# Expert outputs of a mixture-of-experts layer: from a scatter to DRAM and a gather back, to one-hot matmuls that are added to x block by block

## The reference

```python
def hierarchical_moe(h, ...):              # h: 512 tokens x 1024
    g_idx = argmax(h @ w_rg + b_rg)        # 1 of 4 groups
    top_v, top_i = top_k(le[g_idx], 2)     # 2 of its 8 experts
    wts = gate_g * softmax(top_v)
    # the 1024 (token, expert) pairs are sorted by expert
    run_block = (silu(xblk @ w_gate[e]) * (xblk @ w_up[e])) @ w_down[e]   # ff = 512
    out = segment_sum(yb * buf_w, buf_tok)
for i in range(2):
    x = x + mixer_i(rmsnorm(x))
    x = x + hierarchical_moe(rmsnorm(x, norm_ffn_g[i]), ...)
return rmsnorm(x, final_norm_g)
```

## Time and profile before

| | us |
|---|---|
| median of three runs | 1715.41 (1713.95 to 1717.63) |
| the profiled execution, its own time | 1716.26 |
| its span, first to last instruction | 1714.2 |
| expert stage, layer 0 (first gate/up matmul to the end of the last down product) | 477.48 to 939.65 |
| expert stage, layer 1 | 1207.80 to 1685.90 |

### The profile page before, as it was taken

How to read it: one execution, slowest core, us unless ns; L and a number is a source line. 1 busy time by engine, 2 the same in 40 slices (tenths; PEclk the granted TensorE clock), 3 DMA queues, 4 the chain that set the end, 5 groups by cost and what they waited for, 6 DMA issues and landing times. The chain is left out here.

```text
span 1714.2 us, 38730 instructions
## 1 busy us (share of the span) xinstructions
PE 1430.4 (83%) x16146; PEld 929.1 (54%) x16147; DVE 497.1 (29%) x1197; ACT 458.2 (27%) x800; POOL 356.8 (21%) x291
## 2 busy tenths in 40 slices
PE   6999999999796899877588499887977877788883
PEld 5868688686453455444345387565544444445442
DVE  4221121211431222111122779744311211112124
ACT  4242422423321222212122332153212221222222
POOL 3434244342000011100001354520001000001010
PEclk9999999999899999989999699988999998999997
DMA  9212122121779999999999221135499999999985
GB/s 357 99 50 98 50 99 99 49 99 49 294 331 427 429 427 428 428 428 429 429 425 374 99 98 50 52 148 196 170 429 413 413 416 430 427 429 429 416 342 204
DMA packets 39321, 473.83 MB, mean 276 GB/s; under 512 B 6397, under 2 KB 6605, under 8 KB 10849
## 3 DMA queue, kind: packets, MB, share of 16 engines
q1 hardware_dynamic: 34512, 464.42, 65.3%
q0 software_dynamic: 4608, 8.41, 1.3%
q10 hardware_dynamic: 144, 0.17, 0.0%
HBM read 462.48 MB, written 14.68 MB: 278 GB/s over the span
## 5 line engine op out<-in xcount | busy, mean ns | idle before, releaser
L788 PE MATMUL ps<-ring,hgT 128*32 128x256 f32 x6016 | 379.0, 404 | 144.2 <-DMA ring<-w_gu 118.9
L788 PEld LDWEIGHTS ps<-ring,hgT 128*32 128x32 f32 x6016 | 202.4, 115 | 310.3 <-DMA ring<-w_gu 144.9
L437 POOL TENSOR_TENSOR w_lo<-ring,w_hi 128x512 fp32r<-128x512 f32 x176 | 237.5, 1351 | 375.3 <-ACT w_hi L513 375.3
L452 POOL DMA_INDIRECT y_dram<-area_c,idx_s x96 | 94.4, 983 | 781.0 <-ACT area_c L550 761.3
L731 PE MATMUL ps<-area_a,block_rows 128*32 128x256 f32 x3136 | 202.3, 401 | 8.9 <-DVE block_rows L995 8.9
L513 ACT CAST w_hi<-ring 128x512 fp32r<-128x512 f32 x176 | 109.1, 626 | 353.6 <-PE ps L691 353.6
L1117 DVE TENSOR_TENSOR a_e<-sg_e,ps 128x128 f32<-128x128 f32 x94 | 27.1, 288 | 605.8 <-ACT sg_e L545 605.8
L804 PE MATMUL ps<-ring,aT_e 128*32 128x256 f32 x2752 | 166.3, 382 | 25.4 <-DMA ring<-w_down 12.7
L731 PEld LDWEIGHTS ps<-area_a,block_rows 128*32 128x32 f32 x3136 | 111.0, 117 | 83.4 <-issue 26.0
L689 PE MATMUL ps<-w_hi,hT_hi 128*128 128x512 f32 x320 | 126.0, 394 | 7.2 <-DVE hT_lo L1296 7.2
L545 ACT ACT_TABLE_LOAD x94 | 120.6, 1283 | 40.7 <-DVE wts L1111 39.0
(11 more groups left out here) (199 smaller groups left out, 1508.2 us busy)
## 6 DMA issues: line engine op xcount, KB each, us to landing
ring<-w_gu SPq DMA_DIRECT2D x128, 2048.0 KB, 19.0
ring<-w_down SPq DMA_DIRECT2D x58, 2048.0 KB
ring<-w_pw SPq DMA_DIRECT2D x6, 2048.0 KB, 10.9
ring<-w_qk SPq DMA_DIRECT2D x4, 2048.0 KB
ring<-w_v SPq DMA_DIRECT2D x4, 2048.0 KB, 8.2
ring<-w_g SPq DMA_DIRECT2D x4, 2048.0 KB
ring<-w_out SPq DMA_DIRECT2D x4, 2048.0 KB
area_c<-w_down SPq DMA_DIRECT2D x2, 2048.0 KB, 12.6
```

Of the source, the lines that this page charges most:

```text
L437: nc.gpsimd.tensor_tensor(w_lo[:, place, :], ring[:, s, at:at + 512], w_hi[:, place, :].bitcast(F32), ALU.subtract).then_inc(lo_ready, 1)
L452: pool.indirect_dma_start(y_dram[l], bass.IndirectOffsetOnAxis(ap=idx_s[:, b:b + 1].bitcast(U32), axis=0), y_out[:, b, :], None, bounds_ch ...
L788: last = nc.tensor.matmul(ps[32 * g:32 * g + 32, 2, 0:256], hgT[:, n * (KT // 2) + k, :], gate_up[n][:, k, :, g * P:(g + 1) * P], start=(n ...
```

## The change

Nothing goes through DRAM any more. After each block, four one-hot row tiles bring its output to x:

- ACT and DVE write the output, times its routing weight, as the sum of two fp32r parts, `y_hi` (ACT) and `y_lo` (DVE).
- POOL makes `slot_tok` (128 x 512): 1 where slot p of the block holds token t.
- PE does `put_rows` twice per block (halves of 256 tokens): 16 matmuls in fp32r with K = 32 rows, 128 output columns and 256 moving columns each, in four row groups of the array, group g to PSUM bank 4 + g. They run one block late: in block t they move the output of block t-1. The first half stands behind gate/up, the second behind the down product.
- DVE adds each 128 x 1024 row tile from four banks to x (`add_tile`, four per block).
- Picking is one block ahead instead of two, behind the first half of `put_rows`.
- The ring has nine slots, three experts deep (`DEPTH = 3`); the places of the spare down matrices became slots 6 to 8. Now expert 2 is loaded before the stage, nine loads of 96 as before.
- The routing weights are worked out earlier, and the table matmul (L772) has 216 columns in place of 72. After the last block there are two more halves of `put_rows` and four adds, in place of the transfers and `combine`.

```diff
+        places = [ring[:, n, :] for n in range(NSLOT)] + \
+            [area_c[:, 0:SLOT], area_b[:, 0:SLOT], hT[:, :, :].rearrange("p k s -> p (k s)")]
-        slots_of = [(0, 1, 2), (3, 4, 5)]
+        slots_of = [(0, 1, 2), (3, 4, 5), (6, 7, 8)]
@@ SP
-                        upto = sp.value_load(cum[0:1, bass.ds(2 * pair + (odd - 1), 1)], min_val=1, max_val=NBLK - 1)
+                        upto = sp.value_load(cum[0:1, bass.ds(DEPTH * turn + (n - 2), 1)], min_val=1, max_val=NBLK - 1)
-                sp.wait_ge(rows_out[l], 1)
-                for i in range(NT):
-                    sp.dma_start(ytile[i], y_dram[l].rearrange("(t r) c -> t (r c)", r=8)[i * P:(i + 1) * P, :]) \
-                        .then_inc(y_loaded[l][i], 16)
@@ POOL
+                with pool.Fori(0, total) as t:
+                    pool.wait_ge(tok_hot[l], t + 1)
+                    pool.nop(nofuse=True)
+                    pool.tensor_copy(slot_now[:, :], slots[:, bass.ds(t, 1)]).then_inc(slot_known[l], 1)
+                    pool.wait_ge(slot_known[l], t + 1)
+                    pool.wait_ge(second_mm[l], t + 1)
+                    pool.nop(nofuse=True)
+                    nc.gpsimd.tensor_scalar(slot_tok[:, :], tok_number, slot_now[:, 0:1], None,
+                                            ALU.is_equal).then_inc(tok_hot[l], 1)
@@ ACT
                     act.wait_ge(y_mm[l], t + 1)
-                    act.wait_ge(y_free[l], t + 1)
-                    nc.scalar.copy(area_c[:, bass.ds((t % GRP) * QW + 4096, QW)], ps[:, 4, 0:QW]) \
-                        .then_inc(y_ready[l], 1)
+                    act.wait_ge(second_mm[l], t + 1)
+                    nc.scalar.activation(y_hi[:, :], ps[:, 3, P:P + QW], ACT.Copy,
+                                         scale=slots[:, bass.ds(t + NBLK, 1)]).then_inc(y_rounded[l], 1)
@@ PE
+            def put_rows(half, bank, done):
+                for i in range(2):
+                    cols = slice((2 * half + i) * P, (2 * half + i + 1) * P)
+                    for n, part in enumerate((y_hi, y_lo)):
+                        for g in range(4):
+                            rows = slice(32 * g, 32 * g + 32)
+                            last = nc.tensor.matmul(ps[:, bank + g, i * QW:(i + 1) * QW], slot_tok[rows, cols],
+                                                    part[rows, :], start=(i == 0 and n == 0), stop=(i == 1 and n == 1),
+                                                    tile_position=(32 * g, 0))
+                last.then_inc(done, 1)
...
-                pick_rows(l, t + 2)
+                pe.wait_ge(y_split[l], t + 1)
+                pe.wait_ge(tok_hot[l], t + 1)
+                pe.wait_ge(added[l], 4 * t + 4)
+                put_rows(0, 4, first_mm[l])
+                pick_rows(l, t + 1)
                 pe.wait_ge(act_ready[l], t + 1)
                 nc.tensor.transpose(ps[:, 3, 0:P], a_e[:, :], ident).then_inc(t2_mm[l], 1)
                 turn_block(l, t + 1)
...
                 last.then_inc(y_mm[l], 1)
+                pe.wait_ge(added[l], 4 * t + 6)
+                put_rows(1, 4, second_mm[l])
@@ DVE, loop over the blocks
-                    dve.wait_ge(gu_mm[l], t + 1)
+                    dve.wait_ge(first_mm[l], t + 1)
+                    add_tile(0, 4).then_inc(added[l], 1)
+                    stage(l, t + 1)
+                    add_tile(1, 4).then_inc(added[l], 1)
                     turned_block(l, t + 1, gain)
-                    stage(l, t + 2)
-                    know_rows(l, t + 3)
+                    know_rows(l, t + 2)
+                    dve.wait_ge(y_rounded[l], t + 1)
+                    V.scalar_tensor_tensor(out=y_lo[:, :], in0=ps[:, 3, P:P + QW],
+                                           scalar=slots[:, bass.ds(t + NBLK, 1)], in1=y_hi[:, :].bitcast(F32),
+                                           op0=ALU.mult, op1=ALU.subtract).then_inc(y_split[l], 1)
+                    dve.wait_ge(second_mm[l], t + 1)
+                    add_tile(2, 4).then_inc(added[l], 1)
+                    add_tile(3, 4).then_inc(added[l], 1)
```

More of the change, by code:

```diff
@@ L159, in program @@
         slot_hot_r = over("slot_hot_r", [P, 8, P], trig_at, 0)
-        block_hot_r = over("block_hot_r", [P, 8, NBLK], area_c_at, route_at)
+        block_hot_r = over("block_hot_r", [P, 3, 8, NBLK], area_c_at, route_at)
+        y_hi = over("y_hi", [P, QW], area_c_at, route_at)
+        y_lo = over("y_lo", [P, QW], area_c_at, route_at + QW)
+        slot_tok = over("slot_tok", [P, S], area_c_at, route_at + 2 * QW)
         ident = const[:, C_ID:C_ID + P]
@@ L201, in program @@
         eq = room[:, 784:912].rearrange("p (i e) -> p i e", i=NT)
-        block_hot = room[:, 576:1152].rearrange("p (j b) -> p j b", j=8)
-        work = room[:, 1440:1696].rearrange("p (j e) -> p j e", j=8)
-        table = room[:, 1696:1696 + NBLK]
+        block_hot = room[:, 1152:1728].rearrange("p (j b) -> p j b", j=8)
+        work = room[:, 0:256].rearrange("p (j e) -> p j e", j=8)
         group_hot = room[:, 1768:1784].rearrange("p (i g) -> p i g", i=NT)
@@ L807, in one_block @@
                 last.then_inc(y_mm[l], 1)
+                pe.wait_ge(added[l], 4 * t + 6)
+                put_rows(1, 4, second_mm[l])
             def experts(l):
-                with pe.Fori(0, SPARE[0] // 2) as pair:
-                    for odd in range(2):
-                        slots = slots_of[odd]
-                        first = pe.value_load(cum[0:1, bass.ds(2 * pair + odd, 1)], min_val=0, max_val=NBLK - 2)
-                        after = pe.value_load(cum[0:1, bass.ds(2 * pair + (odd + 1), 1)], min_val=1, max_val=NBLK - 1)
+                with pe.Fori(0, LOOPED // DEPTH) as turn:
+                    for n in range(DEPTH):
+                        slots = slots_of[n]
+                        first = pe.value_load(cum[0:1, bass.ds(DEPTH * turn + n, 1)], min_val=0, max_val=NBLK - 2)
+                        after = pe.value_load(cum[0:1, bass.ds(DEPTH * turn + (n + 1), 1)], min_val=1, max_val=NBLK - 1)
                         with pe.Fori(first, after) as t:
-                            one_block(l, t, pair, *slots)
-                for e in range(SPARE[0] // 2 * 2, NE):
+                            one_block(l, t, turn, *slots)
+                for e in range(LOOPED, NE):
                     first = pe.value_load(cum[0:1, e:e + 1], min_val=0, max_val=NBLK - 2)
@@ L1014, in stage @@
                 dve.wait_ge(pick_mm[l], t + 1)
[L1015 removed]
+                V.tensor_copy(hg[:, :], ps[:, 0, 0:QW]).then_inc(staged[l], 1)
             def route(l, gain):
@@ L1098, in route @@
                 dve.wait_ge(idx_mm[l], 1)
-                link.done(V.tensor_scalar(table, ps[:, 7, 0:NBLK], 0.0, BIG, ALU.is_equal, ALU.mult))
-                link.done(V.tensor_tensor(table, table, ps[:, 7, 0:NBLK], ALU.add))
-                V.tensor_scalar(idx[:, :], table, 4.0, const[:, C_QOFF:C_QOFF + 1],
-                                ALU.mult, ALU.add).then_inc(idx_ready[l], 1)
-                dve.wait_ge(exp_ready[l], 2)
-                link.done(V.tensor_reduce(gate[:, :], group_exp.rearrange("p (i g) -> p i g", i=NT), AX, ALU.add))
@@ L1107, in route @@
-                link.done(V.reciprocal(gate[:, :], gate[:, :]))
-                link.done(V.tensor_scalar(second[:, :], expert_exp, 1.0, None, ALU.add))
-                link.done(V.reciprocal(second[:, :], second[:, :]))
-                link.done(V.tensor_tensor(wts[:, 0, :], second[:, :], gate[:, :], ALU.mult))
-                V.tensor_tensor(wts[:, 1, :], wts[:, 0, :], expert_exp, ALU.mult).then_inc(wts_ready[l], 1)
-            def expert_blocks(l, gain):
+                link.done(V.tensor_copy(slots[:, NBLK:2 * NBLK], ps[:, 7, 2 * NBLK:3 * NBLK]))
@@ new lines, in route @@
+                link.sent(V.tensor_tensor(slots[:, NBLK:2 * NBLK], slots[:, NBLK:2 * NBLK], ps[:, 7, NBLK:2 * NBLK],
+                                          ALU.add))
+                link.done(V.tensor_copy(slots[:, 0:NBLK], ps[:, 7, 0:NBLK]))
+                V.sem_inc(idx_ready[l], 1)
+                link.sent(V.tensor_scalar(y_hi[:, :], const[:, 0:QW], 0.0, None, ALU.mult))
+                link.sent(V.tensor_scalar(y_lo[:, :], const[:, 0:QW], 0.0, None, ALU.mult))
+                link.done(V.tensor_scalar(slot_tok[:, :], const[:, 0:S], 0.0, None, ALU.mult))
```

216 lines of the change are left out of this document (97 added, 119 removed).

## The result

| | before | after |
|---|---|---|
| median, us | 1715.5 (4 runs) | **1772.9** (1767.0 to 1781.6, 4 runs) |
| profiled execution, its span | 1716.3, 1714.2 | 1770.1, 1768.2 |
| layer 0's expert stage | 462.2 | 496.5 |
| layer 1's expert stage | 478.1 | 514.0 |

The changed kernel is slower: ratio 1.0338, 95% interval 1.0291 to 1.0385. The forecast was 1724, so the direction held and the size did not: 49 us are missing from the sum.

A forecast was written before the change was run, and what follows sets the result against it. Transfers bound the expert stages before the change, PE after it. Stages with DVE's place +28.6, tails -18 and starts -1.5 gave +9 on the median 1715.4, so 1724 us, range 1665 to 1806.

The forecast's parts named there:

- PE becomes the bound: Expert stages: PE's sums of 472.5 and 491.9 us exceed the transfers' 426 plus their start.
- Halves, 0.85 each: One half of `put_rows` on PE: 0.45 stream, 0.24 in and out, 0.11 first load, 0.05 waits; 0.85 us.
- Picking one ahead, 0.25: Staging of picked rows now falls between picking and the turn, so down waits for the turn: 0.25 us per block.
- Block, 9.70: One block on PE in the expert stages: 7.75 + 1.70 + 0.25 = 9.70 us.
- DVE's place: Behind the second half, DVE's work may outlast gate/up's cover: 0.15 for 30 blocks following one of the same expert, 4.5 us.
- Change of expert, 22 x 0.67 + 10 x 1.16: Added to each stage's blocks: 0.67 us per change of expert, 1.16 where PE's outer loop turns, as in the earlier kernel.
- Tails, -18: From each layer's last down product to its last norm: about 16 and 17.6 us, gaining 10.1 + 7.8 = 18.
- Starts, -1.5: Before each layer's first gate/up: picking of block 1 leaves the front, 0.8 us earlier; 1.5 for both.
- Cheap halves: Rival for `put_rows`: no stop between tilings, first load prefetched; half 0.5, block 9.0, about 1656 us; chance 0.20.
- DVE or POOL: Rival: `slot_tok` at 5 us or adds at 2 put 1.5 to 2 on a block; about 1880 us; chance 0.08.
- Single file: Rival for `put_rows`: 128-column loads of four row groups can't go together; half 2.05, block 12.1, 1950 us; chance 0.07.
- no overlap in a row group: Rival for `put_rows`: loads wait for their own row group's matmul; half 1.28, block 10.55, 1804 us; chance 0.13.

The follow-up runs named there:

- run 14: Not a label: "that run" is the changed kernel with one read more per expert, 1865.3 us; 14 counts its waits near 2.4 us followed by lower-clock blocks.

## Why the prediction was right or wrong

The direction, the new bound and the block came as forecast; the size did not: +9 forecast, +57 measured. The forecast's own range, 1686 to 1762 for a block between 9.3 and 10.1, does not hold 1772.9, though the block was 9.65. The wide range of 1665 to 1806 holds it only because it also took in a rival that didn't happen, the one without overlap in a row group. That is luck.

*PE becomes the bound*: right. No wait for `ring` in either stage, DMA shares 0.92 and 0.85. (The second run of nines in the DMA row has nine slices, not ten; nothing hangs on it.)

*Halves, 0.85 each*: 0.79 (0.12 ahead of the first load and 0.67 behind it, where the sign named was 0.7 to 1.0). The stream of 0.45 holds by the run without `y_lo`, which took 0.23 off a half.

*Picking one ahead, 0.25*: right. Now the turn starts 0.61 behind the transpose and not 0.17, and down 0.15 sooner behind the turn: 0.3, and the run with two ahead gave 0.30 back.

*Block, 9.70*: 9.65, so 94 blocks came 4.7 us cheaper than the sum had it. The sum also counted the half behind the last down product twice, in the block and in the tail: 1.4 us in both layers.

*DVE's place, 4.5 us*: in part. From gate/up to the first half it takes 3.69 in a block that follows one of the same expert, and 3.59 behind a change of expert: 0.1 for 30 blocks, 3 us.

*Change of expert, 22 x 0.67 + 10 x 1.16 in "Stages"*: **this is the step that failed.** (It also has 32 changes a layer, where 32 experts make 31; that is 1.3 us in all.) The price was carried over from the kernel before as if it were a property of the loop. It is the difference between a chain of the sequencer (1.93, 2.45) and the work queued in front of it, and the change put 32 short instructions there in place of long ones. It measured 1.31 for 42 changes, 1.83 for 18 turns, and 1.44 for the two that leave the outer loop: 91 us, where the sum had 53. The signs were in the earlier trace rows: 0.50 and 1.00 of "issue" in front of gate/up, which I priced and did not ask the cause of.

*Tails, -18*: -16.5, from 9.3 and 7.2 where 10.1 and 7.8 stood; the last norm ends 16.0 and 18.1 behind the last down product, as named. *Starts, -1.5*: nothing; 477.66 for 477.48.

Between the spans the miss is 54.0 - 9.2 = 44.8: the changes 38, tails and starts 3.1, less 4.7 and 1.4 for the blocks and 1.5 for DVE's place. The 11 that remain are the seven blocks at the lower clock, each 1.3 to 1.8 longer than its like: 11.5. Two of them are the first of their layer; the other five, 8.4 of it, stand behind turns with bare waits of 1.7, and with the loop's end moved back, where the waits are 0.91 at most, these five are gone. The last 4 of the 49 lie between the profiled execution and the median.

*The rivals.* Cheap halves: fell, a half is 0.79 and not 0.5. DVE or POOL: fell, the long adds take 1.21 and `slot_tok` 1.56 in the mean over all blocks. Single file and no overlap in a row group: fell by the rows below. Weight loads of `put_rows` in the changed kernel, four in each line, every fourth into the same rows:

```profile
593.05 0.19 PEld L740 LDWEIGHTS ps<-y_lo,slot_tok 32*128 32x128 f32 x4
593.17 0.19 PEld L740 LDWEIGHTS ps<-y_hi,slot_tok 32*128 32x128 f32 x4
593.29 0.20 PEld L740 LDWEIGHTS ps<-y_lo,slot_tok 32*128 32x128 f32 x4
593.62 1.45 PEld L689 LDWEIGHTS ps<-area_a,block_rows 128*32 128x32 f32 x32
```

A set of four follows another by 0.12, while the matmuls of the set before run in the same rows (0.28 to 0.29 each). The rule of the Trainium skill's "TensorE: Matmul & The Clock Gate", Part 3, that a load overlaps running matmuls only in another row group, would make it about 0.22, an estimate with the prediction's 0.11 for a set of loads. The measurement decides, and it is against the rule here.

## What to carry to other kernels

The idle time at a loop's end is not a constant of the loop. It is the sequencer's chain of reads and branches less the time that the work already queued lasts. So look at what stands last before a loop turns: here the 16 short matmuls of a half, with their loads, left 0.72 us of cover and long matmuls 1.46, and moving the short ones to the head of the next turn gave 52 us back. When work moves across the loop's end, read the sequencer's own records and work out the cover anew. And a pause that was free under a transfer bound has its full price, and can have the clock's with it, once the engine itself is the bound.

## What the runs showed that I had not expected

The lead of PE's sequencer is the same at every loop's end of a kernel and differs between kernels. In the changed kernel all 88 ends of the inner loop that the trace records began with 12 loads and 12 matmuls not yet started, 0.72 us, and so did those of the runs with a read more, a read fewer and picking two ahead. In the kernel before and in the one without `y_lo` it was mostly 17 loads and 20 or 21 matmuls, 1.46 us. So neither one count of instructions nor one time describes both, and why they differ stays open.

In the run with one more read, PE idle for 2.38 us was followed by a stretch at a mean granted clock of 0.65, PE idle for 1.85 at the same kind of place by one at 1.00. Lengthening the waits by 0.67 so cost twice its length. The length of a wait alone doesn't decide: in that run 14 of the 18 bare waits near 2.4 us were followed by a block at the lower clock and 16 of the 43 near 1.9; in the changed kernel it was 5 of the 18 near 1.75, and none of those near 1.2.
